# Even mixer rebuilt: scores on 64-row tiles, windowed attention features by tokens and one tile later, norms by statistics, and the tails reordered

## Time and profile before

| what | us |
|---|---|
| median of 3 runs (1285.04 to 1287.56) | 1285.34 |
| the profiled execution, own time | 1283.91 |
| its span | 1282.1 |
| PE busy | 1250.3 |
| POOL busy | 598.9 |
| DVE busy | 462.7 |
| ACT busy | 432.9 |

### The profile page before, as it was taken

One profiled execution on the slowest core, in us unless ns is written; L12 is line 12 of the kernel. 1 busy time (PEld: TensorE's weight loads), 2 busy tenths in 40 slices (PEclk: granted clock), 3 DMA queues, 4 the chain that ended last, 5 costly groups with the idle time before them and its releaser, 6 DMA issues.

```text
span 1282.1 us, 16970 instructions
## 1 busy us (share of the span) xinstructions
PE 1250.3 (98%) x7104; PEld 1027.5 (80%) x7104; DVE 462.7 (36%) x763; ACT 432.9 (34%) x600; POOL 598.9 (47%) x286
## 2 busy tenths in 40 slices
PE   9999999999999999998999999999999999999997
PEld 7878877888888888886777878887788888888885
DVE  5548945211111000115687955553521101010105
ACT  4174623322222221224453355452422222221111
POOL 4241243964444443445743346364595444435341
PEclk9999999999999999999999999999999999999999
DMA  9321032333333233231344342022233333324221
GB/s 305 99 67 66 1 115 84 99 99 99 98 99 99 83 121 125 99 96 49 98 110 124 99 100 92 26 67 99 66 99 99 99 99 99 99 82 134 80 99 65
DMA packets 109375, 122.98 MB, mean 96 GB/s; under 512 B 22386, under 2 KB 84148, under 8 KB 109300
## 3 DMA queue, kind: packets, MB, share of 16 engines
q1 hardware_dynamic: 101828, 118.59, 29.4%
q10 hardware_dynamic: 7472, 3.31, 1.0%
HBM read 117.96 MB, written 3.70 MB: 95 GB/s over the span
## 4 chain that ended last, share of the span: by engine, by line
PE 86%; DVE 7%; POOL 3%; issue 3%; DVEq 1%; ACT 1%; ACTq 0%; POOLq 0%
PE bank L1562 26%; PE bank L1563 26%; PE bank L1564 26%; PE bank L1893 3%; POOL w_lo L638 2%; DVE f_ab L1083 1%; DVE KH L1355 1%; DVE OO L1333 1%; DVE SS L1331 1%; PE bank L1608 1%; DVEq L435 1%; PE bank L1721 0%; PE bank L1845 0%; DVE x_tm L1106 0%; PE bank L1782 0%
## 5 line engine op out<-in xcount | busy, mean ns | idle before, releaser
L638 POOL TENSOR_TENSOR w_lo<-w_raw,w_hi 128x1024 fp32r<-128x1024 f32 (+1 forms) x200 | 470.0, 2374 | 495.3 <-ACT w_hi L768 495.3
L1562 PE MATMUL bank<-x_hi,w_hi 128*128 128x512 f32 x928 | 364.3, 393 | 7.5 <-DVE f_ab L1083 4.0
L1564 PE MATMUL bank<-x_hi,w_lo 128*128 128x512 f32 x928 | 361.7, 390 | 0.0
L1563 PE MATMUL bank<-x_lo,w_hi 128*128 128x512 f32 x928 | 361.6, 390 | 0.0
L768 ACT ACTIVATE w_hi<-w_raw 128x1024 fp32r<-128x1024 f32 (+1 forms) x200 | 196.3, 1031 | 218.3 <-issue 167.3
L1562 PEld LDWEIGHTS bank<-x_hi,w_hi 128*128 128x128 f32 x928 | 174.6, 188 | 46.9 <-issue 8.4
L1564 PEld LDWEIGHTS bank<-x_hi,w_lo 128*128 128x128 f32 x928 | 174.5, 188 | 36.6
L1563 PEld LDWEIGHTS bank<-x_lo,w_hi 128*128 128x128 f32 x928 | 174.5, 188 | 35.4
L1150 DVE TENSOR_TENSOR f_ab<-bank,f_ab 128x512 f32<-128x512 f32 x44 | 30.4, 691 | 368.9 <-PE bank L1564 368.9
L1563 PE MATMUL bank<-w_lo,h_hi 128*128 128x512 f32 x352 | 140.4, 399 | 0.0
L1562 PE MATMUL bank<-w_hi,h_hi 128*128 128x512 f32 x352 | 138.7, 394 | 0.0
(11 more groups left out here) (270 smaller groups left out, 1179.5 us busy)
## 6 DMA issues: line engine op xcount, KB each, us to landing
w_raw<-ffn_w_gate_dram SPq DMA_DIRECT2D x22, 1024.0 KB, 5.3
w_raw<-ffn_w_up_dram SPq DMA_DIRECT2D x22, 1024.0 KB, 5.3
w_raw<-ffn_w_down_dram SPq DMA_DIRECT2D x20, 1024.0 KB, 5.0
w_raw<-od_w_in_dram SPq DMA_DIRECT2D x16, 1024.0 KB, 5.9
w_raw<-ev_w_in_dram SPq DMA_DIRECT2D x8, 1024.0 KB, 5.9
w_raw<-ev_w_out_dram SPq DMA_DIRECT2D x4, 1024.0 KB, 5.1
w_raw<-od_w_out_dram SPq DMA_DIRECT2D x4, 1024.0 KB, 5.1
x_fm<-x_fm_dram SPq DMA_DIRECT2D x8, 256.0 KB, 6.7
```

Of the source, the lines that this page charges most:

```text
L638: pool.tensor_tensor(w_lo[:, b % 2, c], w_raw[:, b % 2, c], w_hi[:, b % 2, c].bitcast(F32), ALU.subtract).then_inc(w_lo_ready, 1)
L1562: pe.matmul(out_ap, st[0], mv_[0], start=start, stop=False)
L1563: pe.matmul(out_ap, st[0], mv_[1], start=False, stop=False)
L1564: return pe.matmul(out_ap, st[1], mv_[0], start=False, stop=stop)
```

## The change

Even mixer. k is kept as 64 rows twice (`k_twice`: the head's 64 features in both halves) and needs two transposes a tile. Scores of even and odd heads come from the upper and the lower 64 rows, into one bank each. The probabilities are divided by their sum on POOL before they are transposed; the windowed output is made features by tokens, so it is not transposed again, and one tile later (`turn_probs(t - 1)`, `windowed(t - 1)`); `turned` names its bank as the second half of the output. gattn keeps only the two diagonal 64 x 64 blocks of each head. gout's mean and variance come from bn_stats and bn_aggr, its scaling from four products. gr's projection is cut in three pieces. POOL splits the first block of mix inside its last tile. The tail order and the release of a half-0 block's buffer (`w_used`) are written out.

LayerNorms. z is normalised and announced in halves; for even k ACT makes `x_hi` straight from the bank and then `f_ab`, DVE makes `f_ab` of odd k and all of `x_lo`; PE's fresh block takes the four products with `x_hi` first. The ring of six banks begins two units later (at `ba_fm` instead of the first conv), and `ba` comes one convolution later.

Odd mixer. Another bank order and unit order in tile 0; qk before `small_blocks` in the others; in the last tile DVE scales and gates in one operation and POOL does nothing; mix fillers are cut and interleaved with the last transposes.

```diff
+LAST_FILLERS = {0: [("mix", 0, 0, 2)], 1: []}
+def turned(layer, t, i):
+    return ("sout", t) if (layer, i) == (0, 1) else ("oT", layer, t, i)
...
         if t == 0:
-            u += filler(-1) + gram + both("kTM", "vTM") + filler(0) + both("qk") + filler(1) + m1 + filler(2) + ds
+            u += filler(-1) + gram + both("kTM") + filler(0) + both("vTM", "qk") + filler(1) + m1 + filler(2) + ds
         else:
-            u += gram + both("kTM", "vTM") + m1 + ds + both("qk") + filler(1) + both("kS")
+            u += gram + both("kTM", "vTM") + m1 + both("qk") + ds + filler(1) + both("kS")
...
-        if key == ("conv", CONV_ORDER[0]):
+        if key == ("ba_fm",):
             ring, turn = list(range(6)), 0
...
         elif key == FILLERS[0, -1]:
-            ring, turn = [0, 1, 2, 3, 6, 7, 4, 5], 0
+            ring, turn = [0, 6, 7, 1, 2, 3, 4, 5], 0
...
+                        if t == NT - 1:
+                            split_lo(b + 1)
+                        pool.wait_ge(s["s_den_ready"], t + 1)
+                        for e in range(2):
+                            p = s_p[:, t % 2, e, :].rearrange("p (h n) -> p h n", h=4)
+                            den = s_den[:, t % 2, e:QH:2].unsqueeze(2).broadcast_to([P, 4, P])
+                            pool.tensor_tensor(p, p, den, ALU.mult).then_inc(s["s_weight"], 1)
...
+                for k in range(0, KD, 2):
+                    full(act, ("xT", i, k))
+                    src = bank(("xT", i, k))[:, :]
+                    g, v = lnc[:, gcol + k:gcol + k + 1], lnc[:, gcol + 16 + k:gcol + 17 + k]
+                    act.activation(x_hi[:, k, :], src, ACT.Identity, scale=g, bias=v).then_inc(s["x_hi_ready"], 1)
...
+                    take(act.activation(f_ab[:, k % 4, :], src, ACT.Identity, scale=g, bias=v), ("xT", i, k))
...
+                for h in range(GH):
+                    ins = dve.bn_stats(g_st[:, h, :], k4(key)[:, h, :])
+                link(ins)
+                for h in range(GH):
+                    ins = dve.bn_aggr(g_mv[:, h, :], g_st[:, h, :])
+                ins.then_inc(s["o_var"], 1)
+                if t:
+                    round_o(0, t - 1)
                 dve.wait_ge(s["o_rstd"], t + 1)
                 link(dve.reciprocal(g_var[:, :], g_var[:, :]))
-                link(dve.tensor_tensor(og, og, across(g_var[:, :], GDV), ALU.mult))
+                for h in range(GH):
+                    ins = dve.tensor_scalar(o_tm[:, t % 2, h * GDV:(h + 1) * GDV], k4(key)[:, h, :], g_mv[:, h, 0:1],
+                                            g_var[:, h:h + 1], ALU.subtract, ALU.mult)
...
+                for h in range(4 * hg, 4 * hg + 4):
+                    ins = dve.scalar_tensor_tensor(OO[:, h, :], OO[:, h, :], oms[:, h:h + 1],
+                                                   gate_s[:, NT - 1, h * P:(h + 1) * P], ALU.mult, ALU.mult)
...
+                    for n in range(len(keys)):
+                        ps = fill(keys[n]) if k == 0 else bank(keys[n])
+                        w = weights(b, k, n * P, P)
+                        pe.matmul(ps[:, :], w[0], x[0], start=k == 0, stop=False)
+                        pe.matmul(ps[:, :], w[1], x[0], start=False, stop=False)
+                    low_part_there(pe, fresh, k)
...
-                            ins = pe.matmul(ps[c * CH:(c + 1) * CH, hh * P:(hh + 1) * P],
-                                            s_qT[:, h // 2, chunk * CH:(chunk + 1) * CH],
-                                            s_kT[:, 2 * g + h % 2, chunk * CH:chunk * CH + 2 * CH],
+                            ins = pe.matmul(ps[e][c * CH:(c + 1) * CH, j * P:(j + 1) * P],
+                                            s_qT[dims, j, chunk * CH:(chunk + 1) * CH],
+                                            s_kT[dims, j // 2, chunk * CH:chunk * CH + 2 * CH],
                                             start=True, stop=True)
...
-                tile_of(("gr", t))
+                gr = ("gr", t)
+                tile_of(gr, 0, 3)
+                if t:
+                    turn_probs(t - 1)
+                    turn_o(0, t - 1)
+                tile_of(gr, 3, 6)
+                if t:
+                    windowed(t - 1)
                 ps = fill(("gattn", t))
                 for h in range(GH):
-                    ins = pe.matmul(ps[:, h * P:(h + 1) * P], g_k[:, h // 2, tile_cols[t]],
-                                    q_pad[:, h, tile_cols[t]], start=True, stop=True)
+                    for c in range(2):
+                        cols = slice(t * P + c * CH, t * P + (c + 1) * CH)
+                        ins = pe.matmul(ps[c * CH:(c + 1) * CH, h * CH:(h + 1) * CH], g_k[:, h // 2, cols],
+                                        q_pad[:, h, cols], start=True, stop=True)
...
                 chunk_state(t, 1)
+                tile_of(gr, 6, 8)
...
+            for key in TAIL_FILLERS[0]:
+                tile_of(key, 0, 4)
+            turn_probs(NT - 1)
+            tile_of(TAIL_FILLERS[0][0], 4, 6)
+            windowed(NT - 1)
+            tile_of(TAIL_FILLERS[0][0], 6, 8)
+            tile_of(TAIL_FILLERS[0][1], 4, 8)
             turn_o(0, NT - 1)
+            for k0 in (0, 4):
+                for key in LAST_FILLERS[0] + [last]:
+                    tile_of(key, k0, k0 + 4)
...
+            ahead, last = TAIL_FILLERS[1][0], ("mix", 1, 0, NT - 1)
+            filler(NT - 1, 3, 7, 8)
+            tile_of(ahead, 0, 4)
             turn_o(1, NT - 1)
+            tile_of(ahead, 4, 7)
+            tile_of(last, 0, 4)
+            tile_of(ahead, 7, 8)
+            tile_of(last, 4, 8)
```

More of the change, by code:

```diff
@@ L242, in unit_plan @@
         elif key == FILLERS[0, -1]:
-            ring, turn = [0, 1, 2, 3, 6, 7, 4, 5], 0
+            ring, turn = [0, 6, 7, 1, 2, 3, 4, 5], 0
+        elif key == TAIL_FILLERS[1][0]:
+            free = [slots[k][0] for k in (("ds", NT - 1, 64), ("oT", 1, NT - 2, 0), ("oT", 1, NT - 2, 1))]
+            ring, turn = free + [b for b in ring if b not in free], 0
         if key in held:
             b = held[key]
+        elif key[0] == "gstate" and key[2] == 1 and key[1]:
+            b = slots["probT", key[1] - 1, 0][0]
         else:
@@ L871, in _, with copy_probs @@
             split_to(first_block[("gr",)] + 1)
+            def copy_probs(t):
+                for g in range(KVH):
+                    full(act, ("probT", t, g))
+                    take(act.activation(s_pT[:, g, :], bank(("probT", t, g))[:, :], ACT.Copy), ("probT", t, g))
             for t in range(NT):
@@ L1235, in _ @@
             for t in range(NT):
-                for g in range(KVH):
-                    key = ("score", t, g)
-                    hs = slice(4 * g, 4 * g + 4)
+                for e in range(2):
+                    key = ("score", t, e)
+                    hs = slice(e, QH, 2)
                     full(dve, key)
@@ L1289, in _ @@
+                take(ins, key)
+                taken(dve, key)
                 dve.wait_ge(s["gr_ready"], t + 1)
[L1290 removed]
+                dve.tensor_tensor(o_tm[:, t % 2, :], o_tm[:, t % 2, :], g_r[:, t, :], ALU.mult)\
                    .then_inc(s["o_even"], 1)
[L1292 to L1296 removed]
@@ L1588, in fm_block @@
                 steps = [(n, k) for n in range(len(keys)) for k in range(KD)]
+                for k in range(KD) if fresh is not None else ():
+                    weights_there(b, k)
+                    pe.wait_ge(s["x_hi_ready"], KD * fresh + k + 1)
+                    x = xcols(k, ALL)
+                    for n in range(len(keys)):
[4 more added lines that the diff above has]
+                    low_part_there(pe, fresh, k)
+                    for n in range(len(keys)):
+                        ins = pe.matmul(bank(keys[n])[:, :], weights(b, k, n * P, P)[0], x[1], start=False, stop=k == KD - 1)
+                        if k == KD - 1:
+                            done(ins, keys[n])
                 if fresh is not None:
-                    steps = [(n, k) for k in range(KD) for n in range(len(keys))]
+                    return
                 for n, k in steps:
@@ L1666, in tile_of @@
                               k == 0, k == KD - 1)
+                if key[0] == "mix" and key[-1] == NT - 1 and k1 == 4:
+                    ins.then_inc(w_used, 1)
                 if k1 == KD:
@@ L1699, in have @@
                 def have(k):
-                    taken(pe, ("oT", layer, NT - 1, k // 4))
-                for half in range(2):
-                    tiles = [t for t in range(NT) if ("mix", layer, half, t) not in FILLED]
-                    tm_group(("mix", layer, half), have, in_turn=half == 1, tiles=tiles)
+                    taken(pe, turned(layer, NT - 1, k // 4))
+                tm_group(("mix", layer, 1), have, in_turn=True)
                 turn_x(2 * layer + 1)
@@ L1739, in _ @@
                 pe.wait_ge(s["k_rotated"], t + 1)
-                for j in range(4):
```

(3 more changed lines are left out.)

274 lines of the change are left out of this document (134 added, 140 removed).

## The result

The changed kernel takes 1295.53 us (median; 1294.88 to 1297.86), the kernel before beside it 1285.19: ratio 1.0079, 95% interval [1.0062, 1.0097]. It is slower by 10 us, where 18 us of gain had been forecast. Its profiled span is 1293.9 us against 1282.1.

The account below looks back on a forecast made before the run. TensorE, busy 98% of the span, was taken as the bound. Savings of 1.9 + 4.1 + 1.3 + 6.75 + 0.6 + 1.5 + 2.1 = 18.3 us took 1283.91 to 1265.6, median 1267 us; range 1261 to 1277.

Parts of the forecast that it names:

- step E: LayerNorms 1, 2, 3: z in halves, x_hi straight from the bank, other banks for LayerNorm 2; 6.75 us saved.
- F: Delta rule: 0.6 us from tile 0's kTM wait, 1.5 in tiles 1 to 3, 2.1 in the tail.
- A: Before the even mixer's loop: eight fewer kT transposes and the g_v wait moved behind gattn; 1.9 us saved.
- C: Even mixer loop: PE waits 0.9 us for o_even, tiles 1 to 3 last 15.0 each; 4.1 us saved.
- D: Even mixer's tail, gout(3) to mix: fewer transposes, but new waits of 2.5 and 1.0 us; 1.3 us saved.
- B: PE work of one full even tile: 14.3 us against 16.66, with scores at 1.0.
- rival 2: Even mixer: 64-row products sharing a bank do not overlap, gout's diagonal takes 1.95 instead of 1.05; 1271 us, chance 0.07.
- the rule weighed for it: Different row tiles cannot use the same PSUM bank at once; by it gout's diagonal in the even mixer is serial.
- Rival 5: Even mixer: scores stay at 1.85 us a tile; 1268 us, its chance counted inside the forecast's 0.53.
- Rival 3: Even mixer: new holes absent, o_even in time (0.9 x 3) and POOL's first split hidden (2.5); 1262 us, chance 0.10.
- Rival 4: Even mixer loses the high clock through PE's new idle times; about 1320 us, chance 0.05, of which 0.04 ends slower.
- Rival 1: Even mixer: DVE's chain from gout to o_even, delayed beside POOL's products, decides; 8 us lost, 1275 us, chance 0.25.

Follow-up runs that it names:

- the last experiment: Kernel of 1270.27 us (POOL's split held, both rings turned, gr(3) whole before windowed), with ACT's last-even-tile order and PE's odd-tail order changed: 1268.25 us.
- split held: Changed kernel, but in each LayerNorm POOL splits the second weight block behind the norm only after the last low part of x: 1278.79 us, ratio 0.9946.
- split held and rings turned: Changed kernel with POOL's LayerNorm split after the last low part, and rings from conv group 12 and after the convolutions starting at bank 1: 1271.33 us.
- the rings turned and no hold: Changed kernel with only the rings from conv group 12 and after the convolutions started at bank 1: 1287.49 us, ratio 1.0020.
- the hold released at k 3: Against the kernel of 1271.33 us (both rings starting at bank 1), POOL's split released after the low part of k 3, not k 7: 1280.10 us.

## Why the prediction was wrong, step by step

**The sum** had 18.3 us of gain. After shows 0.9 + 4.8 - 4.4 - 9.2 - 1.2 + 1.6 + 0.1 - 4.4 = -11.8. Of the 30.1 us between them, 16.7 belong to step E, 8.1 to the ring at group 12, 1.8 and 2.0 to the two ends of F, 1.0 to A and 0.6 to C and D.

**A (1.9): half right.** 0.9 came. Eight kT transposes went, but PE now stands 0.6 us for ACT's s_qT at 69.79, a wait the step had not looked for. The number is rough: in the ten kernels that have the change this stage lasts 93.1 to 94.1.

**B (14.3 of work a tile): right.** Scores go from 1.85 to 1.03 us (1.0 forecast), and gattn takes 0.6. PE in order of time, after, answering to the earlier trace rows:

```profile
105.28 0.97 PE L1894 MATMUL bank<-g_v,g_at 64*64 64x128 f32 x13
...
106.16 1.09 PE L1853 MATMUL bank<-s_kT,s_qT 64*64 64x128 f32 x30
107.18 0.44 PE L1861 MATMUL bank<-eye,g_kd 128*128 128x128 f32 x2
```

Gout's diagonal starts at 105.28, and the bulk of the next scores follows at 106.16: 16 records in 0.9 us. At 0.12 each they would have taken 1.9. They start in pairs, less than 0.01 us apart, with a pair every 0.11 us. So the two diagonal positions overlap in one bank, and rival 2 is out. So is, for this pair, the rule weighed for it from the Trainium skill, "TensorEngine Tiling (Array Packing)", section "Restrictions and Gotchas": the measurement decides. (What the prediction adds there on scores and gout is its own inference; the page names neither.) The outputs of the pair lie on different partitions; two row positions writing the same partitions of a bank were not tried. Rival 5 falls as well, with scores at 1.03.

**C (4.1): right in the main, 0.7 too high.** Gout(0) ended 12.7 us after the start, 12.6 forecast. Then tiles lasted 15.4, 15.3 and 15.2 and not 15.0. A part of that is the step's own arithmetic: 14.35 of work less the 4.3 ahead of o_even leaves 10.05 and not 9.9. The waits were these, in tile 1 and in tile 2 (with its like at 139.27 in tile 3):

```profile
111.74 0.66 PE L1745 MATMUL bank<-eye,o_tm 128*128 128x128 f32 x4 [1.18 <-DVE o_tm L1324]
...
124.00 0.50 PE L1597 MATMUL bank<-w_hi,x_hi 128*128 128x512 f32 x1 [0.98 <-DVE x_lo L1117]
```

In tile 1 PE stands 1.2 us at oT instead of the 0.9 worked out, because DVE's path from gout to o_even took 5.6 and not 5.1. In tiles 2 and 3 it is the other way round than forecast: PE stands 1.0 us for gr's bank, which was to lie inside the wait at oT, and has no wait left at oT. Rival 3, no holes, is out. Rival 4 did not come in this kernel, where the granted clock from 94 to 175 was 1.00, but its mechanism exists: behind the hole at gout(3) the clock fell in two other kernels, as said under the table, for 0.8 to 1.0 us each. The forecast's two signs of being wrong (a tile over 16 us, the clock between 94 and 175) both look at the even mixer alone, and neither appeared.

**D (1.3): right, 1.4 came.** The holes of 2.41 and 0.64 us behind gout(3) are those forecast at 2.5 and 1.0, and the last experiment shows that most of the first can be had back by order alone.

**E (6.75): the step that failed, and the largest part of the sum's error.** It priced x_lo at 0.68 on DVE and asked only whether DVE keeps up with PE. It never asked what POOL does once the low parts are taken from it. Without them POOL splits and multiplies at once, beside DVE, and each low part of DVE's waits out a POOL instruction. LayerNorms 1 and 3 lost 8.8 where 1.9 of gain was forecast. With the split held they give 0.96 + 0.99, and LayerNorm 2 with both rings turned gives 4.2 of 4.85: 6.1 of 6.75. So for the edits it named, E was right to 0.1 in LayerNorms 1 and 3 and 0.65 too high in LayerNorm 2, whose stage also holds the moves of ba and of the rings. The cost that it put at nothing (what POOL does with the work gone) was 16.7 us over the kernel.

The clock of LayerNorm 2 belongs to it. The first stretch below is after, 582 to 589; the second is the kernel with split held and rings turned, in the corresponding stretch:

```profile
582.00:589.00 7.00, 6.31 (x17) 4.16 (x18) 6.83 (x5) 4.16 (x6) 6.92 (x3) 0.57 0.51 144
```

```profile
575.00:582.00 7.00, 5.99 (x30) 4.84 (x28) 5.80 (x9) 6.67 (x12) 0.00 (x0) 1.00 0.07 17
```

The 3.5 us hole at f_ab had gone, as E said, but waits of 1.83 and 0.66 us, both from the collision, took its place, and the low level (0.57) stayed. Without POOL beside it the stretch is at 2.4 GHz.

**Not in the sum: group 12 (8.1).** The prediction weighed the ring of six where it begins and not where it ends. A bank is free when its last reader is done, so each reset of a ring has to be looked at against the groups just before it. Following the 13 keys from ba_fm would have shown bank 0 twice running.

**F (0.6 + 1.5 + 2.1): tiles right, the ends not.** Tiles 1 to 3 gave 1.6. Tile 0 lost 1.2 where 0.6 was to be won. Its kTM wait went and PE stood for w_lo and then for the blocks. The last two rows are POOL's first step on the blocks, after and in the kernel with split held and rings turned:

```profile
749.02 0.50 PE L1597 MATMUL bank<-w_hi,x_hi 128*128 128x512 f32 x1 [1.46 <-POOL w_lo L651]
751.35 0.50 PE L1597 MATMUL bank<-w_hi,x_hi 128*128 128x512 f32 x1 [0.67 <-POOL w_lo L651]
768.34 0.69 PE L1969 MATMUL bank<-blocks_in,GA 32*32 32x32 f32 x32 [1.75 <-issue]
...
768.32 1.89 POOL L691 TENSOR_TENSOR SS<-blocks_in,o_own 128x1024 f32<-128x1024 f32 x1 [4.78 <-DMA blocks_in<-t_blocks]
...
748.69 1.89 POOL L692 TENSOR_TENSOR SS<-blocks_in,o_own 128x1024 f32<-128x1024 f32 x1 [3.54 <-DMA blocks_in<-t_blocks]
```

As F said, the DMA of the blocks sets the time of that product, so nothing won ahead of it counts. It also sets the difference between kernels. Counted from the start of the stage, POOL's earlier steps agree within 0.05 us after and in the kernel with split held and rings turned, and the last block lands at 23.5 and 22.2 us; the stage lasts 23.6 and 22.3. In the kernels with the rings turned and no hold, and with the hold released at k 3, it lands at 22.9. So this loss is a late transfer and not a collision of DVE and POOL in this stage. Why the transfer takes longer is open. The tail gave 0.1 of 2.1. F took two orders of PE's work for the bound, but the path is DVE's and ACT's from the last o to x_lo: holes of 0.48 and 0.40 at the transposes stand where 0.24 and 0.57 stood, and moving cover between them changed nothing. One k of mix (three matmuls, 0.7 us) also moved out of tile 3 into this stage. Only the hole at w_lo shrank, from 0.94 to 0.28.

**Rival 1** had the right cause in the wrong place. Its row, a DVE product of 2.13 us beside POOL's split, is this collision. I put it into the even mixer, where POOL's products hardly met DVE's, and gave it 8 us; I did not put it into the LayerNorms, where the change moves POOL's work. Of the 0.05 for rival 4, 0.04 was for ending slower. The kernel did end slower, but by nothing that rival described, so that chance was not earned.

## What to carry over

Work taken off an engine lets that engine's next instruction start sooner. Before pricing the gain, follow that next instruction to where it lands, and look in the trace for what it slows: here it cost 16.7 us, and one semaphore wait in each LayerNorm gave them back. Where banks go round in rings that are reset by name, shifting one start moves the phase of every ring behind it; check each seam against the last few users, and do so again for the repair.

## What the runs showed of the hardware

A DVE operation with two SBUF operands, and the one-operand scaling of z from SBUF, take up to one whole POOL operation longer beside POOL. Two low parts took 4.74 us beside POOL operations of 2.82 and 2.70, three took 7.49; alone 0.63 to 0.70 each. POOL is slowed little: 5.1 to 5.6 for the two pieces of a split, 4.74 alone. DVE's operations that read a bank stay at 0.81. The profile books the blocked time as DVE's busy time, so in its idle columns there is nothing to find: only the duration of a known operation gives it away.

The Trainium skill, "SBUF — State Buffer", section "Who interferes with whom", says why. DVE and GpSimd (POOL) share a port pair under an exclusive lock. DVE instructions with two SBUF inputs contend for it with a GpSimd instruction that reads SBUF, and so can tensor_scalar from SBUF in a two-port mode; whoever issues first holds the pair for the whole instruction, and the other blocks. An operation with its one input from a bank does not take part. The trace agrees: 4.74 for two low parts, 3.04 for two scalings of z (1.00 alone), and 0.81 from a bank beside POOL or not. Which mode an instruction ran in, no trace here shows.
